# Beginning output tiles of the recurrent layer before the attention has ended, and thinning the filler

## What is computed

```python
def odd_mixer(h, w_in, g_cq, w_uq, g_ckv, w_ukv, conv_w, ..., w_out):
    cq, ckv, kr, xr, xg = jnp.split(h @ w_in, [i1, i2, i3, i4], axis=-1)
    ...
    yc = dense_mla(qn, qr, kn, rope(kr), v)            # 8 heads of 64: 512 columns
    yd = rglru_block(xr, xg, conv_w, conv_b, wa, ba, wx, bx, lam)   # 512 columns
    return jnp.concatenate([yc, yd], axis=-1) @ w_out  # 1024 x 1024

x = x + odd_mixer(...)
x = x + sq_relu_mlp(rmsnorm_2(x, norm_mlp[layer]), w_mlp1[layer], w_mlp2[layer])
```

## Time and profile before

| | |
|---|---|
| median of 3 runs | 2480.31 us (2479.41 to 2481.1) |
| the profiled execution's own time | 2482.9 us |
| its span, first to last instruction | 2481.1 us |
| TensorE busy | 2406.2 us (97%) |
| VectorE, ScalarE, GpSimd busy | 1237.4, 953.6, 197.7 us |
| mean granted TensorE clock | 0.989 of full |
| recurrent layer's first score to first matmul on the last head pair | 1921.5 to 2077.2 us |
| residual stage up to the third MLP tile's weights | 2077.2 to 2112.9 us |

### The profile page before, as it was taken

How to read it: one execution, slowest core, us unless ns; L and a number is a source line. 1 busy time by engine, 2 the same in 40 slices (tenths; PEclk the granted TensorE clock), 3 DMA queues, 4 the chain that set the end, 5 groups by cost and what they waited for, 6 DMA issues and landing times.

```text
span 2481.1 us, 28583 instructions
## 1 busy us (share of the span) xinstructions
PE 2406.2 (97%) x11278; PEld 1926.9 (78%) x11278; DVE 1237.4 (50%) x2028; ACT 953.6 (38%) x1594; POOL 197.7 (8%) x147
## 2 busy tenths in 40 slices
PE   8999999999999999999999889999999899999998
PEld 6888888777777787888887667888887677888887
DVE  5533436688554345433436765524444775532432
ACT  4323223465433333323223364413324884431431
POOL 0100100322102000100100200000001100000000
PEclk9999999999999999999999999999999998999999
DMA  4323322211212132323322212322222012333231
GB/s 135 105 91 102 96 91 93 79 52 51 66 62 71 62 115 68 103 87 101 101 80 86 71 43 86 118 94 94 95 93 70 30 45 71 102 102 94 94 95 67
DMA packets 66805, 208.50 MB, mean 84 GB/s; under 512 B 7408, under 2 KB 15856, under 8 KB 66416
## 3 DMA queue, kind: packets, MB, share of 16 engines
q1 hardware_dynamic: 66672, 206.68, 26.3%
HBM read 204.55 MB, written 2.10 MB: 83 GB/s over the span
## 4 chain that ended last, share of the span: by engine, by line
PE 87%; DVE 5%; ACT 4%; issue 3%; DMA 1%; POOL 0%; POOLq 0%; SPq 0%; DVEq 0%; ACTq 0%
PE bank L1703 25%; PE bank L1707 25%; PE bank L1705 25%; PE bank L1839 2%; PE bank L1801 1%; PE bank L1846 1%; ACT whi L1960 1%; DMA wraw<-in_stream 1%; DVE wlo L2255 1%; PE bank L1892 1%; PE bank L1830 1%; PE bank L1743 1%; PE bank L1741 1%; PE bank L1745 1%; PE bank L1867 0%
## 5 line engine op out<-in xcount | busy, mean ns | idle before, releaser
L2255 DVE TENSOR_TENSOR wlo<-wraw,whi 128x1024 fp32r<-128x1024 f32 (+5 forms) x436 | 486.8, 1119 | 536.2 <-ACT whi L1960 535.1
L1703 PE MATMUL bank<-hhi,whi 128*128 128x512 f32 x1744 | 696.4, 399 | 7.8 <-ACT whi L1960 5.1
L1707 PE MATMUL bank<-hhi,wlo 128*128 128x512 f32 x1744 | 684.4, 392 | 2.3 <-DVE wlo L2255 2.1
L1705 PE MATMUL bank<-hlo,whi 128*128 128x512 f32 x1744 | 683.6, 392 | 1.7 <-DVE hlo L2261 1.7
L1960 ACT ACTIVATE whi<-wraw 128x1024 fp32r<-128x1024 f32 (+5 forms) x436 | 409.0, 940 | 497.1 <-PE bank L1707 431.4
L1703 PEld LDWEIGHTS bank<-hhi,whi 128*128 128x128 f32 x1744 | 329.4, 189 | 82.8 <-issue 8.2
L1707 PEld LDWEIGHTS bank<-hhi,wlo 128*128 128x128 f32 x1744 | 328.8, 189 | 76.3 <-DVE wlo L2255 6.2
L1705 PEld LDWEIGHTS bank<-hlo,whi 128*128 128x128 f32 x1744 | 329.7, 189 | 68.6 <-DVE hlo L2261 3.6
L1705 PE MATMUL bank<-mlo,whi 128*128 128x512 f32 x576 | 227.8, 396 | 0.2 <-DVE mlo L2526 0.2
L1703 PE MATMUL bank<-mhi,whi 128*128 128x512 f32 x576 | 227.8, 396 | 0.0
L1707 PE MATMUL bank<-mhi,wlo 128*128 128x512 f32 x576 | 227.7, 395 | 0.0
(11 more groups left out here) (395 smaller groups left out, 3110.3 us busy)
## 6 DMA issues: line engine op xcount, KB each, us to landing
wraw<-in_stream SPq DMA_DIRECT2D x343, 512.0 KB, 3.5
wraw<-in_stream SPq DMA_DIRECT2D x32, 192.0 KB, 2.4
wraw<-in_stream SPq DMA_DIRECT2D x22, 256.0 KB, 2.6
wraw<-in_stream SPq DMA_DIRECT2D x26, 128.0 KB, 2.0
wraw<-in_stream SPq DMA_DIRECT2D x8, 320.0 KB, 2.9
xa<-in_x SPq DMA_DIRECT2D x8, 256.0 KB, 5.6
out<-ya SPq DMA_DIRECT2D x8, 256.0 KB, 2.7
m<-in_mask SPq DMA_DIRECT2D x1, 1024.0 KB, 5.0
```

The source lines that it names most:

```text
L1703: pe.matmul(out, sh, xh, start=first, stop=False)
L1705: pe.matmul(out, sh, xl, start=False, stop=False)
L1707: p = pe.matmul(out, sl, xh, start=False, stop=end and last)
L2255: dve.tensor_tensor(wlo[j][:, 0:L], wraw[i][:, 0:L], whi[j][:, 0:L].bitcast(f32), SUB).then_inc(*lo.up(c))
```

## The change

Head pair 3 becomes the last operand tile: the recurrent tiles are stored as 3 to 6 and pair 3 as 7, and the rows of `o_out` are laid out to match. Three new filler steps begin output tiles 0, 1 and 2 with operand tiles 3 to 6 (12 matmuls each) in the three filler banks; `residual` finishes them with tile 7 (3 matmuls each) and makes the other five whole, as before. The filler rate falls from 1.1 + 1.1 to 1 + 0.95 steps a round.

```diff
-    def residual(nxt, x, keys, hfree, k_from=0):
+    def residual(nxt, x, keys, hfree, k_from=0, begun=()):
         sx = Sum(("h", nxt))
         for n in range(8):
-            t = run(feat(keys(n), x, k_from=k_from))
+            t = run(begun[n] if n < len(begun) else feat(keys(n), x, k_from=k_from))
...
-        put("parts", ("cat", 5, 4 + tl), ("lt", q.i), (("gelu_out", tl),), guard)
-        q.free = (("p_lo", ("cat", 5, 4 + tl)),)
+        put("parts", ("cat", 5, 3 + tl), ("lt", q.i), (("gelu_out", tl),), guard)
+        q.free = (("p_lo", ("cat", 5, 3 + tl)),)
...
-        put("parts", ("cat", 5, p), tb.i, (("odd_back", p),), guard)
+        key = ("cat", 5, p if p < 3 else 7)
+        put("parts", key, tb.i, (("odd_back", p),), guard)
         o.free = (("odd_back", p),)
-        tb.free = (("p_hi", ("cat", 5, p)), ("p_lo", ("cat", 5, p)))
+        tb.free = (("p_hi", key), ("p_lo", key))
...
         for _ in old:
             yield
-
+        for n in range(3):
+            begun.append(feat([("oo", n, 0)], ("cat", 5), k_from=3))
+            next(begun[n])
+            yield
+
+    begun = []
     filler["gen"] = stream_odd()
     fill(6)
     rounds([odd_unit(h, i) for h in range(8) for i in range(4)],
-           ((1, 0), (0, 0), (3, 0), (2, 1.1), (1, 1.1)))
+           ((1, 0), (0, 0), (3, 0), (2, 1), (1, 0.95)))
...
-    end = residual(6, ("cat", 5), lambda n: [("oo", n, 0)], (end_h,), 3)
+    end = residual(6, ("cat", 5), lambda n: [("oo", n, 0)], (end_h,), 3, begun=begun)
...
-    w["o_out"] = i["o_w_out_2"][0]
+    oo = i["o_w_out_2"][0]
+    w["o_out"] = np.concatenate([oo[0:384], oo[512:1024], oo[384:512]])
```

## The result

The changed kernel takes 2486.01 us in the median (2483.8 to 2488.61, 13 runs) against 2480.31 (2478.88 to 2482.63, 13 runs): ratio 1.0023, 95% interval 1.0014 to 1.0031. It is slower by 5.7 us, just over the bound of 0.2%, and 3.7 us above the forecast. That lies inside the stated range of 2476.5 to 2487.5, but above the 2479.5 to 2485 of the case that I held likeliest. Its profiled execution took 2488.37 us, with a span of 2486.6.

The account below looks back on a forecast made before the run. TensorE carries 87% of the chain, but VectorE and ScalarE pace the residual stage. +3.7 before T0, -3.5 behind it and +1.8 half clock at the MLP give +2.0 on 2480.3: 2482.3 us, 8-in-10 range 2476.5 to 2487.5.

Parts of the forecast that it names:

- the case that I held likeliest: Whole kernel: the forecast itself, within 2 us or so of 2482.3, own range 2479.5 to 2485; chance 60%.
- Term 1: Before the last operand: three begun tiles put 36 matmuls there, at 0.2333 us each, +8.4 us.
- Term 2: Drain and third pair: waits for ScalarE's copies (2.48 us) and the third pair's 0.45 us operand wait go, together -2.9 us.
- T0: Start of the first matmul that reads the last attention operand; forecast to come 3.7 us later.
- The filling count: Attention rounds: 74 filler steps at 1.95 a round, the last of three new steps landing in the last round.
- TensorE's wait for the fifth chunk: Residual stage: held weight slots delay this chunk's split, so TensorE, ready at T0 + 6.0, idles about 2.8 us.
- VectorE's wait for the seventh: Residual stage: this chunk's transfer starts only after the fifth's low half, 2.90 us wait, holding the fourth add to 14.7.
- the third MLP tile's low half: End of the residual chain: this weight chunk's low-half split ends 32.2 us behind T0 against 35.7, -3.5 us.
- term 4: Middle rounds: thinner filling leaves one more bare round in the first ScalarE-busy stretch, +1.0 us, bounds 0 to 2.7.
- rival C: Middle rounds: thinner filling exposes ScalarE, about 3 us of new waits plus one clock fall, +5 us, 2487.3; chance 18%.
- Term 3: Drain: outputs and transposes run at full instead of half clock once filled, -2.8 us.
- The larger reading: Residual stage: work moves out of a stage TensorE did not bound, so little comes back.

Follow-up runs that it names:

- slots_free: Changed kernel with the last operand's weights of the three begun tiles in a chunk of their own, closing the begun tiles' chunks early; 2480.8 us.
- begun_only: Changed kernel with the filler rate set back to 1.1 + 1.1, keeping the three begun tiles; 2487.4 us.
- after_busy: Changed kernel plus 29 matmuls nobody reads, at the ends of bare rounds 2, 4, 6 and 14 before four middle waits; 2479.0 us.
- before_busy: Kernel before plus unread matmuls (4, 11, 5, 5) at the ends of rounds 2, 3, 5 and 13, before its own middle waits; 2477.1 us.
- slots_busy: Changed kernel with both the separate chunk for the begun tiles' last-operand weights and the unread matmuls in the middle; 2475.1 us.
- rate_only: Kernel before with only the filler rate lowered to 1 + 0.95 steps a round, no begun tiles; 2478.7 us.
- rate_thick: Kernel before with filler rate 1.1 + 1.1 up to round 20 and 1 + 0.4 from there, no begun tiles; 2476.6 us.
- thick_early: Changed kernel with filler rate 1.1 + 1.1 up to round 20 and 1 + 0.6 from there; 2485.1 us.
- rate_busy: Kernel before with filler rate 1 + 0.95 and the same unread middle matmuls as after_busy, no begun tiles; 2471.4 us.
- end_busy: rate_busy with three more unread matmuls behind the last transpose, while the last operand is being split; 2470.3 us.

## Why the prediction was right, and where it was off

**Right, with its sizes.** Term 1: 36 matmuls, and 7.7 us between two kernels that differ in them alone, or 8.1 with the 0.41 us wait that they fill. Term 2: of the four drain waits 0.26 us stayed, behind six filler matmuls that I had held to be enough, and T0's own 0.7 us stayed. The filling count: the last steps landed in the last round. Behind T0, forecast and measured: adds at 1.3, 3.45, 6.2, 14.7 against 1.49, 3.64, 6.38, 14.81; TensorE's wait for the fifth chunk 2.8 against 2.68; VectorE's wait for the seventh 2.9 against 2.91; the third MLP tile's low half 32.2 against 32.3, so -3.4 for -3.5. The half clock followed the 2.92 us wait at the MLP, as in the even layer: from that low half to the norm sums 11.96 us before, 14.22 after, +2.3 for +1.8 (the spell was 6.8 us long and not 3.5). slots_free bears out the mechanism by a price stated ahead (2481.6 against 2480.8); begun_only met its own (2487.6 against 2487.4) with the clock lower for less of the drain and a shorter wait for the fifth chunk than it assumed.

**The step that was mis-sized is term 4, "The filling is thinner in the middle", at +1.0 us.** The stretch to T0 grew by 6.35 us and not 3.7. I priced the extra bare round by a wait; the waits between the first score and the third pair did not grow in sum at all (7.9 us before, by adding up the gaps, 7.4 after). What grew is the time at half clock behind them: 3.4 us before (1937 to 1940), 17 after (1937 to 1943, 1950 to 1954, 1988 to 1995). after_busy shows that this is the term: with the clock held T0 comes 7.57 us earlier than in the changed kernel. This was my rival C in its place and its sign, at 18%, but C too wanted some 3 us of new waits to decide it. It needed none: waits of 3.00 and 1.96 us where there had been 2.72 and 1.16 were enough. The rival's price was 5 us on top of the forecast, 2487.3, and the measured time is 3.7 on top. So the likeliest case as I had it failed in this term, and the range held because it reached out to C.

The terms do not close with this alone. after_busy puts the three spells at 7.6 us and the kernel before paid some 1.7 for its one, so the clock adds about 5.9 where term 4 has 1.0; yet T0 came only 2.65 us later than the sum. The other terms therefore gave back some 2 us more than I had charged. Part of it can be read: a wait costs more than its gap. Two outputs of the drain start 2.23 us apart (2067.33, 2069.56) around a gap of 0.69, where an output and a transpose back to back take 0.84 + 0.44 = 1.28, so this wait costs 0.95. Between first score and T0 the kernel before has 15 waits (11.6 us), the changed one 7 (8.4 us). How the rest divides is open.

**Term 3 was right for the profiled execution and weaker in general.** The drain's half clock was won back, in that trace. But before_busy has the same bare drain with the same waits, and there it stayed at full clock up to T0, and in begun_only to its last output. So the 2.8 us may in part be luck of the one execution that I read, or hang on what came before; one trace of each can't tell. A drain that kept its clock is probably the 1.6 us by which before_busy beat its expectation; it was not tested separately.

**The larger reading holds, and more strongly than I put it.** The work was taken out of a stage that TensorE does not bound and put into one that it does. With the middle's clock held, three begun tiles cost 7.5 us as they were written (2479.0 against 2471.4), of which some 4 is the gathered splits (slots_busy) and 3.6 the move itself. The thin rate, which looked like the price of the change, is its useful half: 5.7 us once the clock is held.

## What to carry to other kernels

Before moving work ahead of a late operand, ask which engine ends the stage that it leaves: if it is not the engine that gets less to do, only the start of that stage moves. A tile left half done holds its weight slot, and splits or loads that were spread over tiles then gather behind it in in-order queues; give the last operand's weights their own piece, or begin only one tile (here that cost nothing, and gained nothing that the runs can tell). When filling is thinned, price the idle time not by its length but by the clock behind it: 29 matmuls that nobody reads, in four waits of 1.0 to 3.0 us that another engine sets, were worth 7 us here.

## What the runs showed of the hardware that I had not expected

- A wait of 3.00 us was followed by 6.8 us of half clock where one of 2.72 us was followed by 3.4; one of 1.96 us by 6.8 us where one of 1.16 us (in other kernels 1.18) by none. In the changed kernel a third spell began at 1950, behind a wait of 1.32 us that had no spell in the kernel before. The other traces with these waits agree (rate_only and slots_free with the changed kernel; begun_only and rate_thick with the one before), but for thick_early, where 1.32 us had a spell of 3.4.
- The length of the wait does not settle it. The wait of 2.67 us for the fifth chunk was followed by no half clock in after_busy, by 3.4 us of it in the changed kernel (2.68) and by 6.8 in thick_early. In the even layer, whose steps none of these kernels changes, the wait of 2.92 us at the MLP was followed by 3.4 us of half clock in the profiled executions of the kernel before and after_busy, and by 6.8 in those of the changed kernel (2.93), rate_only and rate_busy.
- The same bare drain (three waits of 0.69 us, one of 0.41, outputs and transposes between them) fell to half clock in the kernel before and not in before_busy. The 10 us up to that fall (2059.72 to 2069.72) have TensorE busy for 7.94; before_busy, in a stretch of its drain, has the same:

```profile
2060.00:2070.00 10.00, 7.94 (x57) 6.16 (x56) 3.37 (x10) 4.98 (x12) 0.00 (x0) 1.00 0.16 50
```

and the outputs in it are at full speed behind each wait:

```profile
2067.21 1.10 PE L1903 MATMUL bank<-xa,tmps 128*128 128x64 f32 x8 [0.69 <-ACT tmps L2104]
2068.15 0.61 PE L1850 MATMUL bank<-ident,ssb 128*128 128x128 f32 x4
2069.45 1.10 PE L1903 MATMUL bank<-xa,tmps 128*128 128x64 f32 x8 [0.69 <-ACT tmps L2104]
```

So whether a stretch with such waits keeps its clock can't be read from its own waits alone. My estimate, from the 2.8 us of term 3: a sum made from one trace is open by 2 to 3 us for each such stretch.
- With three matmuls (0.7 us) in front of the last operand the first output tile kept the full clock in the profiled execution (first add at T0 + 4.21 in end_busy, 5.75 in rate_busy). That the three did it is not shown: rate_thick kept it there without them, and the medians (2470.3, 2471.4) overlap.
